# Value products in front of the scores in the attention loop of a two-layer streaming encoder

## What is computed

```python
q, k, v = qkv_heads(h, w_qkv)
s = jnp.einsum('bqhd,bkhd->bhqk', q_c, k_c).astype(jnp.float32) * scale + bias
s = jnp.where(valid, s, NEG)
p = jax.nn.softmax(s, axis=-1).astype(v.dtype)
return jnp.einsum('bhqk,bkhd->bqhd', p, v_c)      # then @ w_o
```

## Time and profile before

| what | us |
|---|---|
| median of 3 runs | 2458.02 |
| the profiled execution | 2459.18 |
| its span | 2457.4 |
| PE busy | 2437.5 |
| DVE busy | 1547.0 |
| ACT busy | 907.0 |

### The profile page before, as it was taken

One profiled execution on the slowest core, in us unless ns is written; L12 is line 12 of the kernel. 1 busy time (PEld: TensorE's weight loads), 2 busy tenths in 40 slices (PEclk: granted clock), 3 DMA queues, 4 the chain that ended last, 5 costly groups with the idle time before them and its releaser, 6 DMA issues.

```text
span 2457.4 us, 42975 instructions
## 1 busy us (share of the span) xinstructions
PE 2437.5 (99%) x16495; PEld 2392.1 (97%) x16495; DVE 1547.0 (63%) x2853; ACT 907.0 (37%) x1709; POOL 231.3 (9%) x535
## 2 busy tenths in 40 slices
PE   8999999999999999999999999999999999999998
PEld 8999999999999999999999999999999999999998
DVE  5666666677866666666666734428666666666666
ACT  6555545555333222222233641325222223322223
POOL 1011101113000000000000321221000000000000
PEclk9999999999999999999999999999999999999999
DMA  6122222454111111111111211112111111111012
GB/s 169 54 61 61 63 59 68 135 144 126 52 52 51 51 35 34 50 34 51 51 51 35 71 35 35 49 39 77 44 35 34 51 51 51 51 51 45 34 41 81
DMA packets 136522, 145.37 MB, mean 59 GB/s; under 512 B 4444, under 2 KB 125956, under 8 KB 136420
## 3 DMA queue, kind: packets, MB, share of 16 engines
q1 hardware_dynamic: 120420, 118.69, 15.3%
q0 software_dynamic: 14384, 23.03, 3.6%
q10 hardware_dynamic: 1616, 2.25, 0.3%
HBM read 125.97 MB, written 17.97 MB: 59 GB/s over the span
## 4 chain that ended last, share of the span: by engine, by line
PE 97%; DVE 1%; ACT 0%; DMA 0%; issue 0%; DVEq 0%; ACTq 0%
PE psum L170 29%; PE psum L169 29%; PE psum L171 29%; PE psum L1061 3%; PE psum L1081 2%; PE psum L1026 2%; PE psum L1990 1%; PE psum L919 0%; DMA raw<-in_a_w_qkv 0%; PE psum L1974 0%; DVE raw L2359 0%; PE psum L260 0%; PE psum L2330 0%; DVE w_lo L783 0%; DVE neg_max L1318 0%
## 5 line engine op out<-in xcount | busy, mean ns | idle before, releaser
L169 PE MATMUL psum<-gx_hi,w_hi 128*128 128x352 f32 x3456 | 1123.8, 325 | 1.3 <-DVE gx_lo L231 0.8
L170 PE MATMUL psum<-gx_lo,w_hi 128*128 128x352 f32 x3456 | 1116.3, 323 | 0.0
L171 PE MATMUL psum<-gx_hi,w_lo 128*128 128x352 f32 x3456 | 1115.3, 323 | 0.0
L169 PEld LDWEIGHTS psum<-gx_hi,w_hi 128*128 128x128 f32 x3456 | 649.9, 188 | 3.6 <-issue 1.0
L170 PEld LDWEIGHTS psum<-gx_lo,w_hi 128*128 128x128 f32 x3456 | 649.9, 188 | 0.6
L171 PEld LDWEIGHTS psum<-gx_hi,w_lo 128*128 128x128 f32 x3456 | 649.8, 188 | 0.0
L1749 DVE TENSOR_TENSOR x<-x,psum 128x352 f32<-128x352 f32 x528 | 258.4, 518 | 119.2 <-PE psum L171 118.9
L1620 ACT ACTIVATE conv_t<-a_gate,cur 128x352 f32<-128x352 f32 x132 | 90.0, 681 | 539.6 <-DVE a_gate L1700 532.4
L170 PE MATMUL psum<-h_loB,w_hi 128*128 128x352 f32 x528 | 171.1, 324 | 0.0
L171 PE MATMUL psum<-h_hiB,w_lo 128*128 128x352 f32 x528 | 171.0, 324 | 0.0
L170 PE MATMUL psum<-h_loA,w_hi 128*128 128x352 f32 x528 | 170.9, 324 | 0.0
(11 more groups left out here) (194 smaller groups left out, 2940.8 us busy)
## 6 DMA issues: line engine op xcount, KB each, us to landing
raw<-in_f_w_up SPq DMA_DIRECT2D x44, 1024.0 KB, 5.1
raw<-in_f_w_down SPq DMA_DIRECT2D x22, 1024.0 KB, 4.9
raw<-in_a_w_o SPq DMA_DIRECT2D x25, 512.0 KB, 4.1
raw<-in_a_w_qkv SPq DMA_DIRECT2D x22, 512.0 KB, 4.0
raw<-in_b_w_in SPq DMA_DIRECT2D x8, 1024.0 KB, 5.6
raw<-in_b_w_out SPq DMA_DIRECT2D x4, 1024.0 KB, 5.2
gx_hi<-o_scratch POOLq DMA_DIRECT2D x3, 1232.0 KB, 8.2
gx_lo<-o_scratch POOLq DMA_DIRECT2D x3, 1232.0 KB, 10.7
```

The source lines that it names most:

```text
L169: pe.matmul(out, w[0], rhs[0], start=first, stop=False)
L170: pe.matmul(out, w[0], rhs[1], start=False, stop=False)
L171: return pe.matmul(out, w[1], rhs[0], start=False, stop=last)
```

## The change

In a step that has value products, they and their waits now stand ahead of the scores. Steps without products are as they were, and nothing else is moved. ACT, DVE, POOL and SP have the same instructions in the same order as before.

```diff
         for g in range(ALL + 2):
             t, s = step_of(g)
             third = [2] if 1 <= g <= ALL and len(key_groups((g - 1) % STEPS)) > 2 else []
-            if g < ALL:
+            if g < ALL and not weighed(g):
                 scores(g)
             if weighed(g):
                 at_least(pe, o_out, weighed_to(g))
                 pe.wait_ge(kv_copied, extras_to(min(g, ALL)))
                 pe.wait_ge(kc_lo, cached_to(g))
             for j in weighed(g):
                 weigh(j)
+            if g < ALL and weighed(g):
+                scores(g)
```

## The result

The changed kernel took 2471.32 us (median of four runs, 2471.22 to 2472.23). The kernel before took 2458.15 us beside it (four runs, 2457.92 to 2458.35). That is 13.17 us or 0.54% slower, a ratio of 1.0054 with a 95% interval of 1.0042 to 1.0066. Forecast were 2473.1 us and a range of 2466 to 2479.

What follows compares the result with a forecast made beforehand. PE, busy 99% of the span, was taken to bound the kernel; uncovered copies 12.9, late projections 1.2 and head pair 7 1.0 summed to 15.1 us, forecasting 2473.1 us, 0.6% slower, range 2466 to 2478.9.

Steps and rivals of the forecast that it cites:

- four transposes, no wait before: Seven odd steps behind four transposes: products wait for ACT's 0.60 copy once scores no longer cover it, 0.90 us each.
- s = 6 of t = 1, 3, 5: Query block s = 6, head pairs t: one transpose behind two turns, short copy loses its cover, 0.73 us each.
- s = 0 of t = 1, 3, 5, 7: Query block 0, odd head pairs: products already waited for the copy; scores now come behind, 0.63 us each.
- gaps of the 18 plain steps: Changed steps without transposes ending the step before: gaps between kinds of matmuls only change places, cost 0.
- late projection, s = 8 of even t: Softmax starts later, so the projection waits for DVE's eviction behind the weight split: 0.31 late, four times, 1.2 us.
- head pair 7: Later scores make DVE's bias adds in steps 6 and 8 start 0.45 and 0.55 later; PE waits, 1.0 us.
- c: Time from the end of the last transpose's slot to copy end + 0.10; forecast as the loss, 0.90 or 0.73 us.
- the rule on weight loads that the prediction weighed: Loads hide under running matmuls only where row groups differ, so the scores' load is paid whole: 3.5 us more, 2476.6.
- ACT v or kout: Sign of being right: the profile names this ACT copy as what PE waited for before the products of (1, 4).
- softmax holds the turns: Rival: value-product copies on ACT and DVE lengthen softmax's chain, 3.6 us more, 2476.7; chance 0.10.
- The rival in which later idle time takes the stalls in: From 545 us on, PE's 9.2 us idle could give back up to 9.2 of 15.1: 2463.9; chance 0.06.
- the copies are ready in time: Not-slower rival: products' waits are met when PE arrives and one gap goes per step, 3.1 us less, 2454.9; chance 0.05.

Runs made afterwards that it cites:

- the last experiment: Changed kernel with early transposes and DVE's eviction ahead of the weight split, plus scores ahead of products again in head pair 7: 2456.74 us, ratio 0.9994 to the kernel before.

## Why the prediction was right, and the terms that were off

The mechanism held: PE bounds the loop, the scores were the cover of ACT's copies, and without it PE waits. By the prediction's own steps:

| step | forecast us | measured us |
|---|---|---|
| four transposes, no wait before | 7 x 0.90 = 6.3 | 7 x 0.80 = 5.6 |
| s = 6 of t = 1, 3, 5 | 3 x 0.73 = 2.2 | 3 x 0.62 = 1.9 |
| s = 8 of t = 1, 3, 5 | 3 x 0.63 = 1.9 | 3 x 0.56 = 1.7 |
| s = 0 of t = 1, 3, 5, 7 | 4 x 0.63 = 2.5 | 4 x 0.48 = 1.9 |
| gaps of the 18 plain steps | 0 | -0.01 to 0.01 each (head pair 7 apart) |
| late projection, s = 8 of even t | 4 x 0.31 = 1.2 | 4 x 0.27 = 1.1 |
| head pair 7 | 1.0 | 0.95 |
| sum | 15.1 | 13.1 |

The measured column is the start of the turns of each step, or at s = 8 of even t of the projection, against the same of the kernel before, less what had accumulated until then. The late projection stands in step s = 8 and takes the turns of s = 7, by which the prediction's sum calls it.

The mis-sized term is the gap between products and scores: it was counted twice. "I take 0.09, as the scores there follow full-height work too" added it behind the products' 1.24. But these 1.24 reach from the start of the products to the start of the turns, and so hold the gap behind the products already; that "nothing shows in front of the turns" was misread. A window so narrow that it shows only the last records of the products makes it visible, first in the kernel before, then in the changed one:

```profile
140.97 0.28 PE L1081 MATMUL psum<-pT,v 128*64 128x128 f32 x2
141.18 0.33 PE L1061 MATMUL psum<-ident,pA 128*128 128x128 f32 x1
```

```profile
142.13 0.27 PE L1081 MATMUL psum<-pT,v 128*64 128x128 f32 x1
142.34 0.41 PE L1026 MATMUL psum<-k_hi,q_hi 64*128 64x320 f32 x2
```

Forty records of products take 2.40 and twenty take 1.31, so a product, which is two records, follows another after 2 x (2.40 - 1.31) / 20 = 0.11. What comes behind the last one starts 0.21 after it in both kernels, turns or scores, so a gap of 0.09 to 0.10 stands there in both. Only the gap in front of the scores went into the wait for the copy. The loss of a step is therefore c - 0.09, 0.81 and 0.64, not c. That is 17 x 0.08 = 1.4 of the 1.8 that the copies were over, as 0.01 (1.25 against 1.24) was due where 0.09 was added. About half of the rest is the block of scores at s = 0, 0.48 where I took the 0.54 of the sample's.

By the rule on weight loads that the prediction weighed (the Trainium skill, "TensorE: Matmul & The Clock Gate", Part 3), 3.5 us more would have been due by its estimate. The runs show none of it: the scores start as long behind the products as the turns did, and the plain steps, at 0.00 outside head pair 7, lose nothing. The load of the first score does start with that score's row in both kernels, and that row is 0.10 longer than the next (0.41 against 0.31); this is the same in either order.

Two steps were right in size and not in their signs. I said that the trace would name ACT v or kout for the products' wait; it names "issue", as the earlier trace rows already did for the short wait there. The first product asks for four semaphores at once; why the profile names no engine for them was not tested. The wait is read from the copy's end instead: in all 17 steps the products start 0.10 behind it. And head pair 7's 0.95 was placed at two bias adds of DVE, 0.45 and 0.55; it came in five pieces. The bias adds of steps 6 and 8, and the filler that waits for DVE's residual add (0.47, as before), answer to the earlier trace rows:

```profile
521.71 0.43 PE L169 MATMUL psum<-gx_hi,w_hi 128*128 128x352 f32 x1 [0.47 <-DVE x L1343]
...
529.59 0.70 DVE L1316 TENSOR_TENSOR psum<-psum,bias 128x512 f32<-128x512 f32 x1 [0.92 <-PE psum L1026]
...
544.00 0.49 DVE L1316 TENSOR_TENSOR psum<-psum,bias 32x320 f32<-32x320 f32 x1 [0.38 <-PE psum L1026]
```

Against the earlier trace rows the adds come 13.42 and 13.77 later (529.59 - 516.17, 544.00 - 530.23). PE's loss is 0.18 and 0.16 at the fillers of steps 3 and 7, 0.19 at step 5 (for ACT's exponentials), 0.30 at step 6 (the second set of products for a copy of turned probabilities) and 0.08 at step 8. I read them as one lateness of the ring PE, DVE, ACT that shows wherever PE comes round to it. Shown is, by the last experiment, that the order within head pair 7 causes the loss; the ring itself is argued. The places were wrong, so that the size of 1.0 came out near is in part luck.

Two head pairs take 240.16 - 115.71 = 124.45 us, 3.55 more than the 120.90 of the earlier trace rows, where 4.1 was forecast and 5.5 would have meant that softmax holds the turns. It did not outside head pair 7: the plain steps lost nothing. The rival in which later idle time takes the stalls in falls with the second stretch, which is as long as before. That the copies are ready in time falls with the seventeen waits.

## What to carry to other kernels

Before two blocks on the bounding engine change places, ask of each what it waited for and what ran meanwhile: the block in front is cover for the other's producer, and the loss is the producer's end plus the hop to PE less the end of the work before, step by step. A time from the start of one kind of matmul to the start of the next already holds the gap between them, so a sum made of such times must not add that gap again. Where a consumer stands close behind its producer's copy, look first at moving the producer earlier: here the transposes ahead of the projection gave back 12.0 of the 13.2 that the order had cost, and left 2.6 between the two orders (2459.31 against 2456.72).

## What the runs showed of the hardware

PE starts 0.10 after the end of an ACT copy that it waits for, in all 17 steps (by the rounded rows 141.00 to 141.09, 115.61 to 115.71, 171.23 to 171.32). A gap of 0.09 to 0.10 stands where the kinds of matmuls change between projection and scores (126.41 to 126.50), projection and products (127.86 to 127.95), and, once 0.11 for the last product is taken off, products and turns (140.97 to 141.18) and products and scores (142.13 to 142.34); it is the same whether scores or turns come behind the products. Weight loads of the projection take 188 ns each over the full height while its matmuls start 0.16 apart, and PE and PEld are busy for 99% and 97% of the span at once: loads do lie under matmuls of the same rows there.
